# Moving the SBUF homes of a matmul kernel's operands: rows of 516 elements, and shifts of 4 to 192 bytes

## The chip, the cores and the metric

The kernel runs on 1 core of a Trainium2 chip. The metric is the device time of one execution in microseconds. Two runs of the kernel before took 1668.82 and 1669.12 us, median 1668.97 us.

## The reference

Two transformer blocks run one after the other on x (512 tokens, 1024 channels, fp32), two layers in each. What costs time is the projections, all of them matrix products of a 1024-channel (or 2816-channel) activation with fp32 weights:

```python
def conv_ffn(h, w_up, w_dw, b_dw, w_down):
    u = h @ w_up                      # 1024 -> 5632
    u = causal_dwconv(u, w_dw, b_dw)
    gate, val = jnp.split(u, 2, axis=-1)
    return (jax.nn.silu(gate) * val) @ w_down   # 2816 -> 1024

# first block, per layer l
h = rmsnorm(x, g_mix[l])
# layer 0: h @ w_in_a -> gated causal conv of 31 taps, layernorm, silu
# layer 1: h @ w_in_b, hk @ w_kvf -> attention with forget gates, 12 heads
# both: attention of 4 heads over a memory of 256 rows
x = x + jnp.concatenate([mix, mem_o], axis=-1) @ w_out[l]
x = x + conv_ffn(rmsnorm(x, g_ffn[l]), w_up[l], w_dw_f[l], b_dw_f[l], w_down[l])

# second block, per layer l
proj = jnp.einsum('bsd,de->bse', rmsnorm_2(x, pre_g[l]), w_in[l])
# -> a gated spatial mixing (8 heads) and grouped-query attention with rotary tables (8 heads)
x = x + rmsnorm_2(jnp.einsum('bse,ed->bsd', y, w_out[l]), post_g[l])
```

## The kernel before

**A unit.** All weights come as a stream of 255 units, each 128 partitions x 1024 fp32 elements (512 KB): eight blocks `k` of 128 x 128. A unit u lives in slot u % 4 (`SLOTS = 4`). SyncE loads it into `raw[slot]`, ScalarE rounds it to fp32r into `w_hi[slot]` (L674), GpSimd writes the rest `raw - w_hi` to `w_lo[slot]` (L591). The activations are split in the same way: `xs_hi` and `xs_lo` hold x's high and low part as `[128, 8, 512]` (ScalarE writes the one, VectorE the other), and `hid_hi` and `hid_lo`, `[128, 22, 512]`, hold the hidden layer of the feed-forward part.

**What TensorE does with a unit.** For each of the 8 blocks k it issues three matmuls into one PSUM bank (`products`, L1784): `w_hi` x hi (L1786), `w_hi` x lo (L1787) and `w_lo` x hi (L1788). In each, a weight load puts a 128 x 128 block of `w_hi` or `w_lo` into the array and the matmul streams 512 columns of the activation past it. So TensorE reads two operands of SBUF side by side: the streamed one of the running matmul, and the weight block of the next. 24 such pairs make a unit. `token_products` (L1832 to L1834) does the same with the roles turned: the weights are 128 columns of `xs_hi` or `xs_lo`, and 512 elements of `w_hi` or `w_lo` are streamed. The scores of the second block's attention (L1965, L1966) stream `k_hi` and `k_lo` past `q_stack`.

**Between the units.** Statistics (L1928), transposes (L1942, L1988, L2306), attention and the taps of the convolution (L2058) stand between units or between the blocks k of a unit, on the same TensorE queue, in an order written out by hand. SLOTS - 1 = 3 units are prepared ahead (`AHEAD`).

**Homes.** `put` places every tensor at a running byte address per partition (`cursor`), or at a given one. `LINE = 256`, and three places round the cursor to an address with the remainder of `xs_at` modulo 256: before `mem_kv1` and `k_hi`, and before `h0`, where the region with `hid_hi`, `mem_hi`, `q_stack` and the other stage buffers begins. By the program's addresses `xs_at` is 32896, remainder 128 modulo 256. Rows of 512 elements are 2048 bytes and slots are 4096 bytes, so that every row of `xs_hi`, `xs_lo`, `hid_hi`, `hid_lo`, `mem_hi`, `mem_lo`, `k_hi`, `k_lo` and `q_stack`, and every block of every `w_hi` and `w_lo` slot, begins at remainder 128. `sq_sum` (the weights of L1928) has remainder 0, and `cst` (the identity, the ones) 160.

Of the kernel before, what the change touches and what calls it, by code (L numbers as in the profile page):

```python
# [19 lines left out]
P = 128  # L20
T = 512
TM = 256
D = 1024
KT = D // P
# [13 lines left out]
UNIT = KT * P  # L38
SLOTS = 4
LINE = 256  # L40
AHEAD = SLOTS - 1
N_FOX = 12
N_MEM = 4
N_GQA = 8
# [65 lines left out]
FIRST_PARAMS = 2 * KT  # L110
N_CONSTS = 4 * P + 2 + N_FOX + Q

# [21 lines left out]
def two_blocks(nc, wstream, xT, memT, params, consts, rope, wsT, sbT, post_rows, out):  # L134
    f32, f32r, bf16 = mybir.dt.float32, mybir.dt.float32r, mybir.dt.bfloat16
# [7 lines left out]
    with ctx:  # L143

        start = (nc.sbuf_base + 31) // 32 * 32
        cursor = [start]

        def put(name, shape, dt, at=None):

            size = 4 if dt != bf16 else 2  # L150
            for n in shape[1:]:
                size *= n
            size = (size + 31) // 32 * 32
            where = cursor[0] if at is None else at
            if at is None:
                cursor[0] += size
            return nc.alloc_sbuf_tensor_at(name, shape, dt, offset=where)

        x = put("x", [P, KT, T], f32)
        xs_at = cursor[0]  # L160
        xs_hi = put("xs_hi", [P, KT, T], f32r)
        xs_lo = put("xs_lo", [P, KT, T], f32r)
        raw = [put(f"raw{s}", [P, UNIT], f32) for s in range(SLOTS)]
        w_hi = [put(f"w_hi{s}", [P, KT, P], f32r) for s in range(SLOTS)]
        w_lo = [put(f"w_lo{s}", [P, KT, P], f32r) for s in range(SLOTS)]
        fs_at = cursor[0]
        cursor[0] += 4 * (T + 8) * 4
        u_g = put("u_g", [P, T + 2], f32, fs_at)
# [30 lines left out]
        ident_b = put("ident_b", [P, P], bf16)  # L199
        mask_b = put("mask_b", [P, P], bf16)  # L200
        sel = put("sel", [P, N_FOX], f32r)
        h0 = cursor[0] + (xs_at - cursor[0]) % LINE

        def region():
            at = [h0]
# [15 lines left out]
        headsel = cst[:, 4 * P:4 * P + 2]  # L221
        gate_of = cst[:, 4 * P + 2:4 * P + 2 + N_FOX]
        fold = cst[:, 4 * P + 2 + N_FOX:4 * P + 2 + N_FOX + Q]

# [204 lines left out]
        def attention(name, heads, causal, q_of, k_of, v_of, pt, keys, gates, tile0, read, banks=tight):  # L429
            a = Attention()  # L430
            a.s, a.t, a.o = banks
            a.name, a.heads, a.causal, a.keys, a.gates, a.tile0 = name, heads, causal, keys, gates, tile0
            a.pts = pt
            a.q_of, a.k_of, a.v_of = q_of, k_of, v_of
            a.n = heads // 2 * QT
            a.i0 = sum(b.n for b in attentions)
            a.p0 = sum(b.heads // 2 for b in attentions)
            a.read, a.scale_rows, a.stacked = read, False, False
            attentions.append(a)
            return a  # L440
# [5 lines left out]
        def half(h):  # L446
            return slice(HD * (h % 2), HD * (h % 2) + HD)

        def mem_attention(name, qm, kv, vm, pt, read, banks=tight):
# [12 lines left out]
        att_f = attention(  # L462
            "fox", N_FOX, True,
            lambda h, qt: qf[half(h), h // 2, qt * P:(qt + 1) * P],
# [18 lines left out]
        def steps_in(j):  # L483

            first = KT * (j - ATT_FIRST)
            return [(STEP * s - first, s) for s in range(att_g[0].n + 2) if 0 <= STEP * s - first < KT]

        def b_block(i):

            return (att_m1, i) if i < att_m1.n else (att_f, i - att_m1.n)  # L490
# [97 lines left out]
        def _(pool):  # L588
            def low(s, u):
                pool.wait_ge(unit_hi, u + 1)  # L590
                nc.gpsimd.tensor_tensor(w_lo[s][:].rearrange("p k c -> p (k c)"), raw[s][:],  # L591
                                        w_hi[s][:].rearrange("p k c -> p (k c)").bitcast(f32),
                                        SUB).then_inc(unit_lo, 1)

            def scale_block(a, i):
                nk = keys_of(a, i % QT)
                b = a.i0 + i
                pool.wait_ge(at_inv, b + 1)
                for e in range(2):
                    n = 2 * (b % 2) + e  # L600
                    nc.gpsimd.tensor_scalar(prob[b % 2][:, e, 0:nk], prob[b % 2][:, e, 0:nk], rinv[:, n:n + 1],  # L601
                                            1.0, MUL, MUL).then_inc(at_p, 1)
# [5 lines left out]
            def lows(first, end):  # L608

                n = (end - first) // SLOTS  # L610
                if n >= 2:
                    with pool.Fori(0, n) as g:
                        for j in range(SLOTS):
                            low((first + j) % SLOTS, g * SLOTS + first + j)
                    first += n * SLOTS
                for u in range(first, end):
                    low(u % SLOTS, u)

            def diagonals(t):
                if t >= 2:  # L620
                    pool.wait_ge(part_up, NQ * (t - 1))
                n, w0 = PE_TAPS[t], PARAMS["w_dw_a"] + t * CW + DVE_TAPS[t]
                nc.gpsimd.tensor_tensor(diag[t % 2][:, 0:n, :], fold.unsqueeze(1).to_broadcast([P, n, Q]),
                                        par[:, w0:w0 + n].unsqueeze(2).to_broadcast([P, n, Q]),
                                        MUL).then_inc(diag_ok, 1)
# [12 lines left out]
            for j in range(2 * MT):  # L638
                low((U_GLU + j + AHEAD) % SLOTS, U_GLU + j + AHEAD)
                for k in range(KT):  # L640
# [3 lines left out]
                if 6 <= j < 10:  # L644
                    diagonals(j - 4)
            lows(U_MEM1 + AHEAD, U_B + AHEAD)
            for j in range(B_UNITS):
                low((U_B + j + AHEAD) % SLOTS, U_B + j + AHEAD)
                for k in range(KT):
                    for i in b_steps(j, k):  # L650
                        scale_block(*b_block(i))
            lows(U_OUT1 + AHEAD, U_IN2 + ATT_FIRST + AHEAD)
            for l in range(2):
                u0 = U_IN2 + l * L2_UNITS
                for j in range(ATT_FIRST, IN2_UNITS):
                    low((u0 + j + AHEAD) % SLOTS, u0 + j + AHEAD)
                    for _, i in steps_in(j):
                        if i < att_g[l].n:
                            scale_block(att_g[l], i)
                lows(u0 + IN2_UNITS + AHEAD, min(u0 + L2_UNITS + ATT_FIRST + AHEAD, UNITS))  # L660

# [1737 lines left out]
def _heads_by_pair(n_groups_first):  # L2399

    return [c for t in range(4) for h in (t, t + 4) for c in range(h * HD, (h + 1) * HD)]

def _stream(a):
    import numpy as np
    w_in = a["w_in_a"][0]
    kvf = a["w_kvf"]
    f = np.tile(np.concatenate([kvf[:, 2 * MIX:], np.zeros((D, P // 4 - N_FOX), kvf.dtype)], 1), 4)
    order = _heads_by_pair(4)
# [116 lines left out]
```

## Time and profile before

| | us |
|---|---|
| median of the 2 runs | 1668.97 |
| span of the profiled execution | 1667.2 |
| TensorE matmuls busy | 1636.4 |
| VectorE busy | 856.8 |
| ScalarE busy | 748.9 |
| GpSimd busy | 711.5 |

The mean granted clock of TensorE was 0.997 of full speed. A row of a group of instructions gives line, engine, operation, the tiles written and read (the streamed operand first, then the weights), the shape, the count, and then busy time and the mean length of one in ns. A matmul is 0.39 us long while the next one begins after 0.23 us: they overlap, so what TensorE's work costs is read from one start to the next, not from the length. "PEld" are the weight loads.

### The profile page before, as it was taken

What the parts mean: (1) busy time and instruction counts of PE and PEld (TensorE: products, weight loads), DVE (VectorE), ACT (ScalarE), POOL (GpSimd) and SP (SyncE); (2) the same over time, 40 slices, a digit from 0 to 9 for tenths busy, and PEclk for the clock granted to TensorE, in tenths of its full rate; (3) what the DMA queues carried; (4) which work ended last, traced back from release to release, by engine and by line L of the source; (5) the groups of instructions that cost most, each with busy time, mean ns of one, the idle gap of its engine ahead of it and who ended that gap; (6) DMA issues with size and microseconds to landing.
All of it is one profiled execution on the core that took longest, in us unless ns stands there. A gap on an engine that the chain in (4) does not pass through costs nothing.

```text
span 1667.2 us, 23890 instructions
## 1 busy us (share of the span) xinstructions
PE 1636.4 (98%) x8600; PEld 1290.4 (77%) x8600; DVE 856.8 (51%) x1431; ACT 748.9 (45%) x1189; POOL 711.5 (43%) x406
## 2 busy tenths in 40 slices
PE   8999999999999999999999999999999999999998
PEld 7656788888888877666888888888877778877776
DVE  7887545454431125434466666511365654566554
ACT  6433544444433235444445555423336643545641
POOL 4433334444444544443444444554424433435431
PEclk9999999999999999999999999999999999999999
DMA  7112123332233322111232233333321122311111
GB/s 254 65 52 65 60 92 101 101 100 91 89 112 113 101 90 76 52 52 37 79 113 91 92 94 101 114 101 113 121 75 51 56 72 64 130 66 51 64 55 60
DMA packets 40683, 144.29 MB, mean 87 GB/s; under 512 B 4640, under 2 KB 4640, under 8 KB 40608
## 3 DMA queue, kind: packets, MB, share of 16 engines
q1 hardware_dynamic: 39456, 139.59, 26.2%
q10 hardware_dynamic: 1152, 3.67, 0.7%
q8 instruction: 51, 0.84, 0.2%
q14 instruction: 24, 0.20, 0.0%
HBM read 141.14 MB, written 2.10 MB: 86 GB/s over the span
## 4 chain that ended last, share of the span: by engine, by line
PE 89%; DVE 5%; ACT 2%; issue 1%; DMA 1%; POOL 1%; SPq 0%; DVEq 0%; ACTq 0%; POOLq 0%
PE banks L1786 24%; PE banks L1788 23%; PE banks L1787 23%; PE banks L2005 3%; PE banks L1988 2%; PE banks L1833 2%; PE banks L1834 2%; PE banks L1832 2%; PE banks L2058 1%; PE banks L1970 1%; ACT prob L738 1%; DVE chain L1422 1%; PE banks L1965 1%; PE banks L1966 1%; DMA raw<-wstream 1%
## 5 line engine op out<-in xcount | busy, mean ns | idle before, releaser
L591 POOL TENSOR_TENSOR w_lo<-raw,w_hi 128x1024 fp32r<-128x1024 f32 x252 | 612.1, 2438 | 718.5 <-ACT w_hi L674 718.3
L1786 PE MATMUL banks<-xs_hi,w_hi 128*128 128x512 f32 (+2 forms) x1488 | 595.9, 400 | 4.1 <-DVE xs_lo L1484 1.6
L1788 PE MATMUL banks<-xs_hi,w_lo 128*128 128x512 f32 (+2 forms) x1488 | 577.2, 388 | 0.0
L1787 PE MATMUL banks<-xs_lo,w_hi 128*128 128x512 f32 (+2 forms) x1488 | 576.1, 387 | 0.0
L674 ACT ACTIVATE w_hi<-raw 128x1024 fp32r<-128x1024 f32 x255 | 263.9, 1053 | 267.0 <-PE banks L1788 221.6
L1786 PEld LDWEIGHTS banks<-xs_hi,w_hi 128*128 128x128 f32 x1488 | 280.2, 188 | 70.0 <-issue 15.7
L1788 PEld LDWEIGHTS banks<-xs_hi,w_lo 128*128 128x128 f32 x1488 | 279.7, 188 | 58.2
L1787 PEld LDWEIGHTS banks<-xs_lo,w_hi 128*128 128x128 f32 x1488 | 280.5, 189 | 53.7 <-issue 2.9
L601 POOL TENSOR_SCALAR prob<-prob,rinv 128x512 f32<-128x512 f32 (+3 forms) x144 | 92.3, 653 | 179.4 <-DVE rinv L1271 179.1
L1786 PE MATMUL banks<-hid_hi,w_hi 128*128 128x512 f32 x352 | 136.9, 389 | 0.0
L1787 PE MATMUL banks<-hid_lo,w_hi 128*128 128x512 f32 x352 | 136.9, 389 | 0.0
L1788 PE MATMUL banks<-hid_hi,w_lo 128*128 128x512 f32 x352 | 136.9, 389 | 0.0
L1335 DVE TENSOR_TENSOR x<-x,banks 128x512 f32<-128x512 f32 x16 | 11.0, 687 | 182.3 <-PE banks L1788 182.3
L1309 DVE TENSOR_TENSOR u_v<-banks,rstd 128x512 f32<-128x512 f32 x44 | 30.5, 692 | 127.2 <-PE banks L1788 127.2
L738 ACT ACTIVATE prob<-banks,nmax,head_r 128x512 f32<-128x512 f32 x64 | 49.2, 773 | 82.5 <-DVE nmax L1260 82.4
L780 ACT ACTIVATE t_v<-u_v,par 128x512 f32<-128x512 f32 x44 | 35.9, 816 | 102.5 <-DVE u_v L1309 102.5
L738 ACT ACTIVATE prob<-banks,nmax 128x256 f32<-128x256 f32 (+3 forms) x80 | 39.7, 502 | 88.0 <-DVE nmax L1263 87.8
L1788 PEld LDWEIGHTS banks<-hid_hi,w_lo 128*128 128x128 f32 x352 | 66.1, 188 | 13.8
L1786 PEld LDWEIGHTS banks<-hid_hi,w_hi 128*128 128x128 f32 x352 | 66.1, 188 | 13.7
L1787 PEld LDWEIGHTS banks<-hid_lo,w_hi 128*128 128x128 f32 x352 | 66.1, 188 | 13.6
L1988 PE MATMUL banks<-cst,prob 128*128 128x128 f32 x440 | 63.4, 278 | 4.3 <-POOL prob L601 3.9
L1988 PEld LDWEIGHTS banks<-cst,prob 128*128 128x128 f32 x440 | 48.8, 141 | 22.9 <-issue 12.4
(270 smaller groups left out, 1986.5 us busy)
## 6 DMA issues: line engine op xcount, KB each, us to landing
raw<-wstream SPq DMA_DIRECT2D x255, 512.0 KB, 3.5
x<-xT SPq DMA_DIRECT2D x4, 512.0 KB, 10.2
out<-pt SPq DMA_DIRECT2D x8, 256.0 KB, 2.0
memx<-memT SPq DMA_DIRECT2D x4, 256.0 KB, 5.0
ws_sb<-wsT ACTq DMA_DIRECT2D x2, 512.0 KB, 4.4
rope_sb<-rope ACTq DMA_DIRECT2D x2, 512.0 KB, 6.3
qk<-post_rows ACTq DMA_DIRECT2D x2, 512.0 KB, 3.6
sb_sb<-sbT ACTq DMA_DIRECT2D x2, 256.0 KB, 5.2
```

The costliest lines, as they stand in the source:

```text
L591: nc.gpsimd.tensor_tensor(w_lo[s][:].rearrange("p k c -> p (k c)"), raw[s][:], w_hi[s][:].rearrange("p k c -> p (k c)").bitcast(f32), SUB) ...
L601: nc.gpsimd.tensor_scalar(prob[b % 2][:, e, 0:nk], prob[b % 2][:, e, 0:nk], rinv[:, n:n + 1], 1.0, MUL, MUL).then_inc(at_p, 1)
L674: A(w_hi[s][:].rearrange("p k c -> p (k c)"), raw[s][:], ACT.Copy).then_inc(unit_hi, 1)
L738: A(prob[b % 2][:, e, 0:nk], a.s[b % len(a.s)][:, e, 0:nk], ACT.Exp, bias=nmax[:, n:n + 1], accum_out=rsum[:, n:n + 1], **kw).then_inc(at_ ...
L780: A(dst[:], src[:, 2:T + 2], ACT.Identity, scale=par[:, bass.ds(ch * 3 + (w0 + 2), 1)], bias=par[:, bass.ds(ch + b0, 1)]).then_inc(tap0, 1)
L1786: MM(dst, w_hi[slot][:, k, :], hi, start=start, stop=False)
L1787: MM(dst, w_hi[slot][:, k, :], lo, start=False, stop=False)
L1788: return MM(dst, w_lo[slot][:, k, :], hi, start=False, stop=stop)
L1832: MM(dst, hi, w_rows(w_hi, slot, half), start=start, stop=False)
L1833: MM(dst, lo, w_rows(w_hi, slot, half), start=False, stop=False)
L1988: last = nc.tensor.transpose(a.t[e][:, k * P:(k + 1) * P], prob[b % 2][:, e, k * P:(k + 1) * P], ident)
L2005: last = MM(a.o[n % len(a.o)][half(e), q0:T], a.v_of(2 * p + e, k), pt_of(a, p)[e][:, k, q0:T], start=(k == 0), stop=(k == nt - 1))
```

## The change

Only addresses change. Each row of `xs_hi` and `xs_lo` is allocated with 516 elements, of which 512 are used. The four `w_hi` slots become pieces of one tensor, moved by 0, 8, 64 and 128 bytes; those of `w_lo` by 0, 4, 128 and 192 bytes. The region with `hid_hi` and the stage buffers begins 64 bytes past the rounded address.

```diff
+HI_SHIFTS = (0, 8, 64, 128)
+LO_SHIFTS = (0, 4, 128, 192)
...
-        xs_hi = put("xs_hi", [P, KT, T], f32r)
-        xs_lo = put("xs_lo", [P, KT, T], f32r)
+        xs_hi = put("xs_hi", [P, KT, T + 4], f32r)[:, :, 0:T]
+        xs_lo = put("xs_lo", [P, KT, T + 4], f32r)[:, :, 0:T]
         raw = [put(f"raw{s}", [P, UNIT], f32) for s in range(SLOTS)]
-        w_hi = [put(f"w_hi{s}", [P, KT, P], f32r) for s in range(SLOTS)]
-        w_lo = [put(f"w_lo{s}", [P, KT, P], f32r) for s in range(SLOTS)]
+
+        def weight_slots(name, shifts):
+            cursor[0] += (xs_at - cursor[0]) % LINE
+            base = cursor[0]
+            whole = nc.alloc_sbuf_tensor_at(name, [P, SLOTS * UNIT + max(shifts) // 4], f32r, offset=base)
+            cursor[0] += SLOTS * UNIT * 4 + max(shifts)
+            firsts = [s * UNIT + shift // 4 for s, shift in enumerate(shifts)]
+            return [whole[:, at:at + UNIT].rearrange("p (k c) -> p k c", c=P) for at in firsts]
+
+        w_hi = weight_slots("w_hi", HI_SHIFTS)
+        w_lo = weight_slots("w_lo", LO_SHIFTS)
+        cursor[0] += -cursor[0] % 32
...
-        h0 = cursor[0] + (xs_at - cursor[0]) % LINE
+        h0 = cursor[0] + (xs_at + 64 - cursor[0]) % LINE
```

The instructions, their shapes, their order on each engine and their semaphores are those of before; each line number from 161 on grows (L1786 becomes L1798, L1787 L1799, L1788 L1800). The remainders of the addresses modulo 256, by the program's own addresses:

| operand | before | after |
|---|---|---|
| `xs_hi`, row k | 128 | 128 + 16 k |
| `xs_lo`, row k | 128 | 16 k |
| `w_hi`, slots 0 to 3 | 128 | 128, 136, 192, 0 |
| `w_lo`, slots 0 to 3 | 128 | 128, 132, 0, 64 |
| `hid_hi`, `hid_lo`, `mem_hi`, `mem_lo`, `q_stack`, `k_lo` | 128 | 192 |
| `k_hi`, `x`, `raw` | 128 | 128 |

## Rows read from the trace of the kernel before

**Rows 1.** The page's head and its row of busy time.

```profile
span 1667.2 us, 23890 instructions
PE 1636.4 (98%) x8600; PEld 1290.4 (77%) x8600; DVE 856.8 (51%) x1431; ACT 748.9 (45%) x1189; POOL 711.5 (43%) x406
```

**Rows 2.** The page's chain that ended last, by engine and by line.

```profile
PE 89%; DVE 5%; ACT 2%; issue 1%; DMA 1%; POOL 1%; SPq 0%; DVEq 0%; ACTq 0%; POOLq 0%
PE banks L1786 24%; PE banks L1788 23%; PE banks L1787 23%; PE banks L2005 3%; PE banks L1988 2%; PE banks L1833 2%; PE banks L1834 2%; PE banks L1832 2%; PE banks L2058 1%; PE banks L1970 1%; ACT prob L738 1%; DVE chain L1422 1%; PE banks L1965 1%; PE banks L1966 1%; DMA raw<-wstream 1%
```

**Rows 3.** TensorE's waits, longest first: us in total, times, longest.

```profile
PE banks L2090 <- ACT mem_hi L809: 6.8, 1, 6.8
PE banks L1988 <- POOL prob L601: 3.9, 8, 0.7
```

**Rows 4.** Matmul groups of the whole run by shape: count, busy us, mean ns.

```profile
L1788 PE MATMUL banks<-xs_hi,w_lo 128*128 128x512 f32 x1440 | 562.6, 391 | 0.0
L1787 PE MATMUL banks<-xs_lo,w_hi 128*128 128x512 f32 x1440 | 561.5, 390 | 0.0
L1786 PE MATMUL banks<-hid_hi,w_hi 128*128 128x512 f32 x352 | 136.9, 389 | 0.0
L1833 PE MATMUL banks<-w_hi,xs_lo 128*128 128x512 f32 x128 | 49.8, 389 | 0.0
L1966 PE MATMUL banks<-k_lo,q_stack 128*128 128x512 f32 x64 | 25.1, 392 | 0.0
```

**Rows 5.** Windows view, 300 to 560 us, and two groups within it.

```profile
300.00:560.00 260.00, 260.00 (x1149) 215.29 (x1148) 99.62 (x146) 100.14 (x126) 119.07 (x50) 1.00 0.31 99
...
L1787 PE MATMUL banks<-xs_lo,w_hi 128*128 128x512 f32 x249 | 96.9, 389 | 0.0
...
L1787 PE MATMUL banks<-hid_lo,w_hi 128*128 128x512 f32 x134 | 52.1, 389 | 0.0
```

**Rows 6.** Timeline of TensorE from 591 us: start, length, line.

```profile
591.03 0.39 PE L1786 MATMUL banks<-xs_hi,w_hi 128*128 128x512 f32 x1
591.26 0.39 PE L1787 MATMUL banks<-xs_lo,w_hi 128*128 128x512 f32 x1
591.49 0.40 PE L1788 MATMUL banks<-xs_hi,w_lo 128*128 128x512 f32 x1
591.72 0.95 PE L1928 MATMUL banks<-cst,sq_sum 128*128 128x1 f32 x8
...
592.85 0.39 PE L1787 MATMUL banks<-xs_lo,w_hi 128*128 128x512 f32 x1
...
594.00 0.40 PE L1786 MATMUL banks<-xs_hi,w_hi 128*128 128x512 f32 x1
594.24 0.39 PE L1787 MATMUL banks<-xs_lo,w_hi 128*128 128x512 f32 x1
594.46 0.40 PE L1788 MATMUL banks<-xs_hi,w_lo 128*128 128x512 f32 x1
...
595.15 0.39 PE L1788 MATMUL banks<-xs_hi,w_lo 128*128 128x512 f32 x1
```

**Rows 7.** Timeline of TensorE after the pause at 231 us.

```profile
231.44 0.39 PE L1787 MATMUL banks<-xs_lo,w_hi 128*128 128x512 f32 x1
...
231.67 0.40 PE L1788 MATMUL banks<-xs_hi,w_lo 128*128 128x512 f32 x1
231.91 0.39 PE L1786 MATMUL banks<-xs_hi,w_hi 128*128 128x512 f32 x1
232.13 0.39 PE L1787 MATMUL banks<-xs_lo,w_hi 128*128 128x512 f32 x1
...
233.99 0.28 PE L1928 MATMUL banks<-cst,sq_sum 128*128 128x1 f32 x2
```

**Rows 8.** Timeline and windows view at the lower clock, 65.2 to 67.2 us.

```profile
65.30 0.63 PE L1787 MATMUL banks<-xs_lo,w_hi 128*128 128x512 f32 x1
...
67.01 0.63 PE L1788 MATMUL banks<-xs_hi,w_lo 128*128 128x512 f32 x1
...
65.20:67.20 2.00, 2.00 (x6) 1.52 (x6) 1.81 (x4) 0.49 (x3) 0.00 (x0) 0.50 0.00 0
```

**Rows 9.** The page's groups of the two engines that write the weight slots.

```profile
L591 POOL TENSOR_TENSOR w_lo<-raw,w_hi 128x1024 fp32r<-128x1024 f32 x252 | 612.1, 2438 | 718.5 <-ACT w_hi L674 718.3
...
L674 ACT ACTIVATE w_hi<-raw 128x1024 fp32r<-128x1024 f32 x255 | 263.9, 1053 | 267.0 <-PE banks L1788 221.6
```

## Prediction

> **What bounds the kernel now.** I read the page's busy row first: TensorE's matmuls fill 1636.4 of 1667.2 us, the next engine only 856.8 [rows 1]. The chain that ended last agrees: 89% of the span is TensorE, and the three lines of `products` alone are 24 + 23 + 23 = 70% [rows 2]. TensorE's waits come third: its longest is 6.8 us, once, and the next adds up to 3.9 us in 8 times [rows 3]. So there is no wait to win or to create at first sight; what decides is how far apart two matmuls start. A change of that spacing is paid on the path almost in full, times the number of matmuls.
>
> The spacing has two regimes. In the undisturbed stretch from 300 to 560 us the window holds 260.00 us and 1149 matmuls (those cut by its edges counted in), which is 226.3 to 226.7 ns each, all 389 ns long, with `xs` and with `hid` alike [rows 5]. From 591.03 to 591.49 it is 0.46 / 2 = 230 by two digits, the same thing coarsely read. But behind an interruption the spacing is longer for a while: from 592.85 to 595.15 ten matmuls take 2.30 us, 230.0 ns each [rows 6], and from 231.44 to 233.99 eleven take 2.55 us, 231.8 ns each [rows 7]. Within these, single steps run from 0.22 us (231.91 to 232.13) to 0.24 us (231.67 to 231.91, 594.00 to 594.24), and the lengths from 0.39 to 0.40 us. Since length and spacing grow together, it is the streaming of the columns that is slowed, not the issue. The slots, the operands and the clock (full in the undisturbed window [rows 5]) are those of the fast regime, and all remainders are equal in both. What differs is the moment at which the two reads of SBUF run relative to each other. After some steps the spacing falls back to about 227 and stays there for hundreds of us.
>
> A second sign: at half clock (granted 0.50, the 1.2 GHz level) four steps take 67.01 - 65.30 = 1.71 us, 427 ns each [rows 8]. 512 columns at that clock are 426.7 ns, so nothing is lost there, while at full clock 226.7 is 13.3 ns more than the 213.3 of 512 columns. The loss appears only when both reads run at full rate.
>
> My reading: streamed rows and weight blocks share something in SBUF, the loss depends on how they meet, and with every remainder equal the stream of pairs settles in a repeating pattern at 226.7 ns, near the good end of what the trace shows (about 224 to 236).
>
> **The change part by part.** Nothing is added or removed: the same 8600 matmuls, the same order, DMAs and semaphores. Three effects are to be priced.
>
> (1) *The spacing of the 512-column fp32r matmuls.* There are 3 x 1440 with `xs`, 3 x 352 with `hid`, 3 x 128 with turned roles and 2 x 64 of scores, 5888 in all (one row of each kind stands in [rows 4]). Some run in the disturbed regime already. The mean lengths tell how many: with `hid` and in the turned form 389, as in the undisturbed stretch; with `xs`, unrounded, 561.5 / 1440 = 389.9 and 562.6 / 1440 = 390.7 ns [rows 4] against 96.9 / 249 = 389.2 [rows 5], 0.7 and 1.5 ns more, 1.1 on the mean. Disturbed steps average (2.55 + 2.30) / 21 = 231.0 ns [rows 6, 7], 4.3 over 226.7. So 1.1 / 4.3 = 26% of the 4320 are disturbed, 3200 are not; with 1056 + 384 and half of the 128 scores, 4700 matmuls are in the good pattern. After the change the difference of remainders changes with k, with the slot and between `w_hi` and `w_lo`, so no two successive pairs meet alike and there is no single pattern to settle in. I take for them the mean of the wandering steps, 231.0: 4700 x 4.3 ns = 20.2 us. Bounds from the rows: all at the shortest step, 224 (0.22 in [rows 7]), 5888 x -2.7 = -16 us; all at the longest, 236 (0.235 to 0.24), 4700 x 9.3 = +44 us. A bound further off is no loss at all, 427 / 2 = 213.4 ns from the half clock [rows 8]: 5888 x -13.3 = -78 us. I take the wandering mean because it is measured on these very shapes at full clock; the half clock is a state the kernel is hardly in.
>
> The premise that remainders matter has one thin piece of evidence. At 591.49, out of the good pattern, the matmul beside which the weights of L1928 are read (`sq_sum`, remainder 0, the others 128) is 0.40 long instead of 0.39 [rows 6]. The weights there are plain fp32 as well, so it could be the type.
>
> (2) *Writes to moved addresses.* ScalarE's 1053 ns and GpSimd's 2438 ns per unit are 3.5 us, in series [rows 9], against 24 x 226.7 = 5.44 us of TensorE per unit, with three units ahead. GpSimd idles 718.5 us before this very line [rows 9]. Cost 0, hidden behind TensorE's unit. It would end only if GpSimd's subtraction grew beyond 5.4 us, 2.2 times its present length; no row shows a start off a 16-byte boundary on any engine, and a copy of the same bytes is the nearest row. The same slack makes the splits of `xs` harmless in the dense stretches; at the edges of stages a tenth more on 8 writes would be below 1 us.
>
> (3) *Blocks that straddle a boundary.* Slots moved by 4 or 8 bytes (one in four of each kind) touch one more piece of memory per block of 512 bytes: at most 1 in 32 pieces more to read, on a weight load whose 188 ns fit into the spacing. I take 0.
>
> Sum, against the profile's own time: 1667.2 + 20.2 = 1687.4 us. The median of the runs is 1.8 us above that span, so 1689 us, 1.2% slower.
>
> The Trainium skill speaks against this. "TensorE: Matmul & The Clock Gate", "Step-by-step: what each phase is for", says that the streamed operand and the weight load have read ports of their own and that loading the next weights takes nothing from the running matmul. By that, addresses would not matter and the time would be 1669. The same page ("Phases on the wall clock") has 215.7 ns between 512-column matmuls; this trace shows 226.7, 11 ns more in a stream with a weight load beside each matmul. The trace disagrees with the page at full clock and would agree with it at half clock, which is why I don't follow it.
>
> **The rivals.**
>
> *A. Addresses don't matter.* The two regimes come from moments alone, the pattern at 226.7 is found again whatever the remainders: 1669 us, plus or minus 3. For it: the one sign of a remainder above is also a change of type. 
> *B. The new pairs meet badly most of the time.* Remainders open relations that this trace does not contain, and many pairs sit at 235 to 236 for whole units: from 234 ns on (+7.3 x 4700 = 34 us) the result is over 2% slower; at 236 it is 1667.2 + 44 + 1.8 = 1713 us. For it: steps of 0.24 exist [rows 6, 7]. Against: they never repeat in the trace, a short step follows. 16%.
>
> *C. The new pairs meet well, the kernel gets faster.* The good pattern of now still loses 13.3 ns per matmul; if equal remainders are what makes both reads want the same piece of memory, spreading them takes loss away. From below 226 ns on the mean it decides for faster; at 224 throughout it gives 1669 - 16 = 1653 us, half of the loss gone (220 ns) gives 5888 x 6.65 = 39 us, 1630 us. For it: the half clock shows that streaming without loss exists. Against: the shortest of the steps in the trace is 224, so over 2% needs spacings never seen at full clock. 11%, of which 5% beyond 2%.
>
> **How the numbers follow.** The forecast (1675 to 1702 us) has 50%, A 23%, B 16%, C 11%. The range from 1665 to 1712 holds the forecast, nearly all of A and most of B, 8 in 10; it leaves out C and the tail of B. The three chances go by 2% of the time (33 us), taken as about what a measurement of this kernel can tell from no change: faster 5%, the far part of C; slower 16%, B; within 2%, the other 79%.
>
> **What would show it.** In the window from 300 to 560 us the count of matmuls should fall from 1149 to about 1126 (260 / 0.231), and the mean lengths of L1798 to L1800 rise from 389 to about 393 ns, with several different lengths from matmul to matmul instead of one. If A is right, count and lengths are unchanged; if C, the lengths are below 389. ScalarE's and GpSimd's writes should keep 1053 and 2438 ns, and TensorE's waits stay below 10 us each; a wait of TensorE for `w_lo` would show part (2) wrong. The prediction fails if the mean spacing in that window is not between 229 and 233 ns.

## The result and the profile after

| | before | after |
|---|---|---|
| median of the 2 runs, us | 1668.97 | 1688.53 |
| span of the profiled execution, us | 1667.2 | 1686.8 |
| mean granted clock | 0.997 | 0.999 |

The ratio is 1.012, with a 95% interval of 1.0104 to 1.0136: 1.2% slower, clearly different from no change, and below the 2% of the three chances. The prediction was 1689 us, with a range of 1665 to 1712.

The page after, its busy row (which answers to [rows 1]) and its chain by engine ([rows 2]):

```profile
PE 1656.4 (98%) x8600; PEld 1290.1 (76%) x8600; DVE 824.9 (49%) x1431; ACT 749.2 (44%) x1189; POOL 686.9 (41%) x406
...
PE 91%; DVE 4%; ACT 2%; issue 1%; POOL 0%; DMA 0%; DVEq 0%; ACTq 0%; POOLq 0%
```

The matmuls are busy for 20.0 us more, in the same number, and the span is 19.6 us longer; no other engine's busy time grew by more than 0.3 us. VectorE's fell from 856.8 to 824.9 us, 29.9 of it on two of its lines (L1313 and L1317). VectorE doesn't bound the kernel, and why these two got shorter was not isolated. TensorE's waits are as short as in [rows 3]; the two longest after:

```profile
PE banks L2102 <- ACT mem_hi L821: 6.0, 1, 6.0
PE banks L2000 <- POOL prob L613: 4.2, 9, 0.7
```

The windows view of 300 to 560 us, with two of its groups. As in [rows 5], the first bracket holds the number of matmuls, and the 1.00 near the end is the granted clock:

```profile
300.00:560.00 260.00, 260.00 (x1127) 211.35 (x1126) 100.36 (x147) 99.14 (x125) 112.28 (x49) 1.00 0.31 98
...
L1799 PE MATMUL banks<-xs_lo,w_hi 128*128 128x512 f32 x252 | 99.0, 393 | 0.0
...
L1799 PE MATMUL banks<-hid_lo,w_hi 128*128 128x512 f32 x124 | 48.6, 392 | 0.0
```

1127 matmuls instead of 1149 in the same 260 us, 393 and 392 ns long instead of 389. Read as the prediction read the 1149, that is a mean step of 230.7 to 231.1 ns, inside its 229 to 233. In the timeline of that stretch the starts no longer come at equal steps: 0.23 us from 300.61 to 300.84, but 0.24 from 302.46 to 302.70, with lengths of 0.39 and 0.40 mixed, as in [rows 6, 7] behind an interruption:

```profile
300.61 0.39 PE L1799 MATMUL banks<-xs_lo,w_hi 128*128 128x512 f32 x1
300.84 0.39 PE L1800 MATMUL banks<-xs_hi,w_lo 128*128 128x512 f32 x1
...
302.23 0.40 PE L1800 MATMUL banks<-xs_hi,w_lo 128*128 128x512 f32 x1
302.46 0.40 PE L1798 MATMUL banks<-xs_hi,w_hi 128*128 128x512 f32 x1
302.70 0.40 PE L1799 MATMUL banks<-xs_lo,w_hi 128*128 128x512 f32 x1
```

The groups of the whole run, against [rows 4]:

```profile
L1800 PE MATMUL banks<-xs_hi,w_lo 128*128 128x512 f32 x1440 | 566.4, 393 | 0.0
L1799 PE MATMUL banks<-xs_lo,w_hi 128*128 128x512 f32 x1440 | 566.4, 393 | 0.0
...
L1798 PE MATMUL banks<-hid_hi,w_hi 128*128 128x512 f32 x352 | 138.4, 393 | 0.0
...
L1845 PE MATMUL banks<-w_hi,xs_lo 128*128 128x512 f32 x128 | 50.5, 394 | 0.0
```

Their busy times tell where the time came from, since a matmul that is longer by some ns also moves the next start by about as many (in the window 389 to 393 ns of length, 226.7 to about 231 of step). `xs` x `w_lo` has 566.4 - 562.6 = 3.8 us more, `xs_lo` x `w_hi` 566.4 - 561.5 = 4.9, the third group (L1786, now L1798, from 580.9 to 584.7) 3.8: 12.5 us. The three `hid` groups have 4.2 us more, the three with turned roles 2.2. That is 18.9 of the 19.6 us.

GpSimd's subtraction, [rows 9], got shorter, from 2438 to 2339 ns, and moved nothing, since it waits for ScalarE:

```profile
L603 POOL TENSOR_TENSOR w_lo<-raw,w_hi 128x1024 fp32r<-128x1024 f32 x252 | 587.1, 2339 | 756.6 <-ACT w_hi L686 756.5
```

### The profile page after: what moved, and what is told of

Its sections match the earlier page's. It is cut to its first block, busy times and chain, and to the rows that moved or that the text cites. A ratio compares the mean times of both kernels' runs of the same rounds, so it can differ in the third digit from the quotient of the medians.

```text
span 1686.8 us, 23890 instructions
## 1 busy us (share of the span) xinstructions
PE 1656.4 (98%) x8600; PEld 1290.1 (76%) x8600; DVE 824.9 (49%) x1431; ACT 749.2 (44%) x1189; POOL 686.9 (41%) x406
## 4 chain that ended last, share of the span: by engine, by line
PE 91%; DVE 4%; ACT 2%; issue 1%; POOL 0%; DMA 0%; DVEq 0%; ACTq 0%; POOLq 0%
PE banks L1798 24%; PE banks L1800 24%; PE banks L1799 24%; PE banks L2017 3%; PE banks L2000 2%; PE banks L1846 2%; PE banks L1844 2%; PE banks L1845 2%; PE banks L2070 1%; PE banks L1982 1%; ACT prob L750 1%; DVE chain L1434 1%; PE banks L1977 1%; PE banks L1978 1%; DVE banks L1434 1%
## 5 line engine op out<-in xcount | busy, mean ns | idle before, releaser
L603 POOL TENSOR_TENSOR w_lo<-raw,w_hi 128x1024 fp32r<-128x1024 f32 x252 | 587.1, 2339 | 756.6 <-ACT w_hi L686 756.5
L1798 PE MATMUL banks<-xs_hi,w_hi 128*128 128x512 f32 (+2 forms) x1488 | 599.8, 403 | 3.8 <-DVE xs_lo L1496 1.6
L1800 PE MATMUL banks<-xs_hi,w_lo 128*128 128x512 f32 (+2 forms) x1488 | 581.1, 391 | 0.0
L1799 PE MATMUL banks<-xs_lo,w_hi 128*128 128x512 f32 (+2 forms) x1488 | 581.0, 390 | 0.0
L686 ACT ACTIVATE w_hi<-raw 128x1024 fp32r<-128x1024 f32 x255 | 263.9, 1053 | 274.1 <-PE banks L1800 227.7
L1798 PEld LDWEIGHTS banks<-xs_hi,w_hi 128*128 128x128 f32 x1488 | 279.9, 188 | 74.1 <-issue 15.5
L1800 PEld LDWEIGHTS banks<-xs_hi,w_lo 128*128 128x128 f32 x1488 | 279.5, 188 | 62.7
L1799 PEld LDWEIGHTS banks<-xs_lo,w_hi 128*128 128x128 f32 x1488 | 280.1, 188 | 58.3 <-issue 2.9
L1800 PE MATMUL banks<-hid_hi,w_lo 128*128 128x512 f32 x352 | 138.6, 394 | 0.0
L1798 PE MATMUL banks<-hid_hi,w_hi 128*128 128x512 f32 x352 | 138.4, 393 | 0.0
L1799 PE MATMUL banks<-hid_lo,w_hi 128*128 128x512 f32 x352 | 137.9, 392 | 0.0
L1799 PEld LDWEIGHTS banks<-hid_lo,w_hi 128*128 128x128 f32 x352 | 66.1, 188 | 15.4
L1800 PEld LDWEIGHTS banks<-hid_hi,w_lo 128*128 128x128 f32 x352 | 66.1, 188 | 15.2
L1798 PEld LDWEIGHTS banks<-hid_hi,w_hi 128*128 128x128 f32 x352 | 66.1, 188 | 14.7
```

Source lines behind the costliest of these rows:

```text
L686: A(w_hi[s][:].rearrange("p k c -> p (k c)"), raw[s][:], ACT.Copy).then_inc(unit_hi, 1)
L1798: MM(dst, w_hi[slot][:, k, :], hi, start=start, stop=False)
L1799: MM(dst, w_hi[slot][:, k, :], lo, start=False, stop=False)
L1800: return MM(dst, w_lo[slot][:, k, :], hi, start=False, stop=stop)
```

## The experiments

All kernels are the one before with other homes; none leaves work out. The measured quantity beside the time is the mean length of a 512-column matmul in the window of 300 to 560 us: 389 there means a step of 226.7 ns, and each ns of length is about a ns of step. "Difference" is how many bytes the streamed row begins past the weight block it meets, modulo 256; before the change it is 0 for all of these matmuls.

The expectations weigh these explanations against each other. V is the prediction's own: differences that vary keep the pairs from settling. N: any difference other than 0 costs. S: starts off a 16-byte boundary cost. D: the cost depends on the difference alone. H: the homes of before are special as such. W: it is the weight blocks' start that costs.

### One part of the change at a time

Rows of 516 alone:

```diff
-        xs_hi = put("xs_hi", [P, KT, T], f32r)
-        xs_lo = put("xs_lo", [P, KT, T], f32r)
+        xs_hi = put("xs_hi", [P, KT, T + 4], f32r)[:, :, 0:T]
+        xs_lo = put("xs_lo", [P, KT, T + 4], f32r)[:, :, 0:T]
```

> Only the rows of xs_hi and xs_lo are 516 elements long; slots and hid stay at remainder 128. Theory V (a loss comes from differences of remainders that vary from pair to pair, so that no pattern can repeat): the xs matmuls rise from 389.2 in the dense window to about 393 ns, hid stays at 389; 3500 matmuls x 4.3 ns = +15 us, 1684. Rival S (starts off a 16-byte boundary cost, rows of 2064 bytes being whole 16-byte pieces): 1669, nothing. Rival N (any difference from zero costs, constant or not): as V here.

1686.30 us, ratio 1.0106 (1.0089 to 1.0123). The window's groups:

```profile
L1801 PE MATMUL banks<-xs_lo,w_hi 128*128 128x512 f32 x252 | 99.2, 394 | 0.0
...
L1801 PE MATMUL banks<-hid_lo,w_hi 128*128 128x512 f32 x125 | 48.6, 389 | 0.0
```

V and N had 1684 us, S 1669. In one trace, the matmuls whose streamed operand was moved are at 393 to 394 and those whose streamed operand was not are at 389 as before. Addresses matter (rival A of the prediction falls). All starts here are on 16-byte boundaries, so rival S alone doesn't explain it either.

Slots alone (at the addresses that the diff's shifts give, rows of 512, `h0` as before):

```diff
+HI_SHIFTS = (0, 8, 64, 128)
+LO_SHIFTS = (0, 4, 128, 192)
```

> Only the slots are moved, w_hi by 0, 8, 64, 128 and w_lo by 0, 4, 128, 192; xs rows 512, hid not moved. Within a unit the difference now takes two values in turn, one for w_hi and one for w_lo. Theory V: no settled pattern in slots 1 to 3, which is three quarters of 4700 x 4.3 ns, +15 us, 1684, xs and hid alike at about 392. Rival S: only slot 1 is off a 16-byte boundary, a quarter, +5 us or less. Rival N: slots 1 to 3 again, +15 us.

1686.38 us, ratio 1.0104 (1.0088 to 1.0121), as V and N had it; S had at most 5 us. xs is at 392 to 394, hid too:

```profile
L1801 PE MATMUL banks<-xs_lo,w_hi 128*128 128x512 f32 x253 | 99.2, 392 | 0.0
...
L1800 PE MATMUL banks<-hid_hi,w_hi 128*128 128x512 f32 x124 | 48.8, 394 | 0.0
```

The hid region alone:

```diff
-        h0 = cursor[0] + (xs_at - cursor[0]) % LINE
+        h0 = cursor[0] + (xs_at + 64 - cursor[0]) % LINE
```

> Only the region with hid is moved by 64 bytes: during the 1056 matmuls with hid the difference is a constant 64. Theory V: a constant difference lets the pattern settle; 1669, hid at 389 or another single length. Rival N: every hid matmul loses about 4 ns, hid mean 393, +4 us, 1673. Rival S: 1669, hid 389.

1670.69 us, ratio 1.0013 (1.0004 to 1.0023). The window:

```profile
L1801 PE MATMUL banks<-xs_lo,w_hi 128*128 128x512 f32 x247 | 96.1, 389 | 0.0
L1800 PE MATMUL banks<-hid_hi,w_hi 128*128 128x512 f32 x135 | 53.2, 394 | 0.0
L1802 PE MATMUL banks<-hid_hi,w_lo 128*128 128x512 f32 x134 | 52.5, 392 | 0.0
L1801 PE MATMUL banks<-hid_lo,w_hi 128*128 128x512 f32 x134 | 52.0, 388 | 0.0
```

With hid the pairs do settle, in a repeating group of three: 394, 392, 388, mean 391.3, 2.3 ns over 389. 1056 x 2.3 = 2.4 us against a measured 1.9. So a constant difference can settle, as V says, but at another level and in three lengths, which V had left open.

The three parts don't add: 17.5 + 17.6 + 1.9 = 37 us, and all three together cost 19.6. Rows alone and slots alone each already put the xs matmuls at 392 to 394, and doing both puts them at 393: the loss is a level that is reached, not a toll per edit.

### Four constant differences side by side

`w_hi` and `w_lo` of a slot are moved alike, and each slot has its own name, so that the groups of one trace are an experiment each:

```diff
+HI_SHIFTS = (0, 4, 8, 16)
+LO_SHIFTS = (0, 4, 8, 16)
```

> w_hi and w_lo of one slot are moved alike, slots by 0, 4, 8, 16 bytes, and carry names of their own (a to d), so that one run gives four constant differences side by side. Theory V: each slot settles at a single length after a few matmuls, a at 389, the others possibly at another, and the whole is within 5 us of 1669 unless the settled value is another. Rival N: a 389, b, c and d about 393. Rival S: b and c (4 and 8 bytes) longer, d (16) at 389.

1688.23 us, ratio 1.0117 (1.0097 to 1.0137). Window groups, slots a to d:

```profile
L1800 PE MATMUL banks<-xs_hi,w_hi_d 128*128 128x512 f32 x64 | 25.4, 398 | 0.0
...
L1800 PE MATMUL banks<-xs_hi,w_hi_b 128*128 128x512 f32 x64 | 25.2, 394 | 0.0
...
L1800 PE MATMUL banks<-xs_hi,w_hi_a 128*128 128x512 f32 x64 | 25.0, 390 | 0.0
...
L1800 PE MATMUL banks<-xs_hi,w_hi_c 128*128 128x512 f32 x59 | 23.2, 392 | 0.0
```

Within units of constant difference, 4, 8 and 16 bytes cost 4, 2 and 8 ns on this line, and slot a, with difference 0, is back at 390 between them. V falls in its strict form: it isn't the variation that costs, the 24 pairs of one slot meet alike and still lose. N (each non-zero difference costs) is right here, though the costs differ; S falls too, since slot d, on a 16-byte boundary, is the worst. The sign of the difference has to be kept in what follows: here the weights lie past the row, so these are differences of -4, -8 and -16.

With shifts of (0, 32, 64, 128) and hid moved by 160:

> Slots a to d moved by 0, 32, 64, 128 bytes, hid region by 160: eight constant differences at once, for xs 0, 32, 64, 128, for hid 160, 128, 96, 32. Theory D: each has its own mean between 226 and 233 ns (length 388.5 to 396), a with xs lowest at 389 to 390, 64 near 391. A difference below 389 would be a faster home. Rival N: all but a with xs at 393.

1692.92 us, ratio 1.0147 (1.0127 to 1.0167). Slot a with xs: 389 to 390. All seven other differences: 392 to 396, none below 389. In the window:

```profile
L1800 PE MATMUL banks<-xs_hi,w_hi_a 128*128 128x512 f32 x64 | 24.9, 389 | 0.0
L1801 PE MATMUL banks<-xs_lo,w_hi_c 128*128 128x512 f32 x61 | 24.1, 396 | 0.0
...
L1800 PE MATMUL banks<-hid_hi,w_hi_a 128*128 128x512 f32 x28 | 11.1, 396 | 0.0
```

One expectation was missed: "64 near 391". Slot c with xs is at 395 to 396. The 391.3 came from the hid region moved by 64, where the row lies 64 past the weights; here the weights lie 64 past the row, which modulo 256 is another difference (192).

With shifts of (160, 192, 224, 240) and hid moved by 192:

> Slots a to d moved by 160, 192, 224, 240 bytes, hid region by 192: constant differences for xs of 160, 192, 224, 240, for hid of 32, 0, 32 the other way and 48. Theory D: hid with slot b (difference 0) at 389 to 391 though both stand 192 bytes from xs; the others between 389 and 396. Rival H (the homes of before are special): hid with slot b no lower than the rest.

1689.71 us, ratio 1.0128 (1.0107 to 1.0148). The window:

```profile
L1801 PE MATMUL banks<-xs_lo,w_hi_a 128*128 128x512 f32 x64 | 25.5, 399 | 0.0
...
L1802 PE MATMUL banks<-xs_hi,w_lo_b 128*128 128x512 f32 x64 | 25.2, 394 | 0.0
...
L1801 PE MATMUL banks<-xs_lo,w_hi_b 128*128 128x512 f32 x64 | 25.1, 392 | 0.0
...
L1800 PE MATMUL banks<-xs_hi,w_hi_d 128*128 128x512 f32 x64 | 24.9, 389 | 0.0
...
L1800 PE MATMUL banks<-hid_hi,w_hi_b 128*128 128x512 f32 x30 | 11.7, 389 | 0.0
L1801 PE MATMUL banks<-hid_lo,w_hi_b 128*128 128x512 f32 x30 | 11.7, 389 | 0.0
```

hid with slot b, both 192 bytes past their old homes (remainder 64), is at 389: the homes of before are nothing special (rival H falls), two operands moved by the same 192 bytes are as good. And slot d with xs, whose weights begin 16 bytes before the streamed row modulo 256 (difference 16), is at 389 to 390, as good as equal homes. Slot b with xs has the difference of 64 with the sign that hid had above, and is at 389, 392 and 394, the same three levels. The rest is at 392 to 399, three ns above what was expected for the worst.

### The same constant difference everywhere

```diff
+HI_SHIFTS = (192, 192, 192, 192)
+LO_SHIFTS = (192, 192, 192, 192)
```

> All slots are moved by 192 bytes, so that xs and hid alike stand 64 bytes before or 192 behind the weights modulo 256, everywhere and constantly, which is the difference that hid had in the run with hid alone moved (64). Theory D with a period of 256 bytes: the three repeating steps of 231.7, 229.1 and 225.9 ns found there, mean 228.9, now on 4700 matmuls: 4700 x 2.2 = +10 us, 1679. Rival N (any difference costs 4 to 5 ns): 1688. If the period isn't 256: another pattern, between 224 and 236.

1679.91 us, ratio 1.0070 (1.0053 to 1.0087), against 1679 expected. The hid groups:

```profile
L1800 PE MATMUL banks<-hid_hi,w_hi 128*128 128x512 f32 x129 | 50.8, 394 | 0.0
L1802 PE MATMUL banks<-hid_hi,w_lo 128*128 128x512 f32 x129 | 50.6, 392 | 0.0
L1801 PE MATMUL banks<-hid_lo,w_hi 128*128 128x512 f32 x129 | 50.1, 388 | 0.0
```

394, 392, 388 again, the group of three of the run with hid alone moved by 64. There the streamed row began 64 bytes past the weights, here the weights begin 192 past the row: the same modulo 256. So the pattern depends on the difference modulo 256 (or a divisor of it; against 128 speaks slot c of the shifts 0 to 128, at 395 to 396 with a difference of 192), and its cost grows with the matmuls that have it: 4700 x 2.3 = 10.8 us against a measured 11.4, with the turned roles now unequal too.

### Both operands moved alike, off a boundary

```diff
-        xs_hi = put("xs_hi", [P, KT, T], f32r)
-        xs_lo = put("xs_lo", [P, KT, T], f32r)
+        def moved(name):
+            whole = put(name, [P, KT * T + 1], f32r)
+            return whole[:, 1:1 + KT * T].rearrange("p (k t) -> p k t", t=T)
+
+        xs_hi = moved("xs_hi")
+        cursor[0] += (xs_at - cursor[0]) % LINE
+        xs_lo = moved("xs_lo")
...
+HI_SHIFTS = (4, 4, 4, 4)
+LO_SHIFTS = (4, 4, 4, 4)
```

> xs_hi, xs_lo and all weight slots begin 4 bytes past their homes of before, off every 16-byte boundary, but alike: the difference of remainders is 0 for xs. hid stays, so that with hid the difference is a constant 4 bytes. Theory D (only the difference of the two homes counts): xs settles at 389 and 226.7 ns again, hid is near the 232.4 of the slot moved by 4, 1056 x 5.7 = +6 us, 1675. Rival S (the boundary counts): xs near 232, +20 us and more. Rival H (the homes of before are special as such): the same as S.

1714.66 us, ratio 1.0277 (1.0260 to 1.0294), the slowest of all. The window:

```profile
L1805 PE MATMUL banks<-xs_hi,w_hi 128*128 128x512 f32 x256 | 102.7, 401 | 0.0
L1806 PE MATMUL banks<-xs_lo,w_hi 128*128 128x512 f32 x256 | 102.4, 400 | 0.0
...
L1806 PE MATMUL banks<-hid_lo,w_hi 128*128 128x512 f32 x111 | 43.7, 394 | 0.0
```

Theory D was wrong: with equal remainders 4 bytes off, xs is at 397 to 401, 11 ns over 389 and worse than with any unequal pair above, while hid, streamed from its old home past weights moved by 4, is at 394 as slot b was, as expected, and there the difference is constant over the whole stretch. Of the rivals S comes nearest, with over twice its price. A boundary counts besides the difference. Which boundary, and is it the streamed row's? The next two runs ask this. First the same kernel with 16 instead of 4 bytes:

> xs_hi, xs_lo and all slots 16 bytes past their homes of before, alike; hid stays. Theory D16 (the difference counts, and besides it a streamed row that begins off a 16-byte boundary costs more): xs settles at 389 and 226.7 again; hid, whose weights now stand 16 bytes past it, is near the 233.3 of the slot moved by 16, 1056 x 6.6 = +7 us, 1676. Rival B32 (the boundary is 32 bytes or more): xs loses as with 4 bytes, near 238, 1710 and more.

1691.90 us, ratio 1.0145 (1.0129 to 1.0160). The window:

```profile
L1806 PE MATMUL banks<-xs_lo,w_hi 128*128 128x512 f32 x253 | 99.7, 394 | 0.0
...
L1805 PE MATMUL banks<-hid_hi,w_hi 128*128 128x512 f32 x122 | 48.2, 395 | 0.0
```

For xs neither expectation holds; hid (394 to 397) is where it was expected. xs does not return to 389 (theory D16), nor is it near 400 (B32): 393 to 394. 16 bytes are better than 4, but not a boundary on which equal homes are good; the good pairs of equal homes in these runs stand at remainders of 128 and 64, both multiples of 64. Whether equal homes 32 bytes off would do was not tried. With unequal ones a row at remainder 32 was no worse than others: hid in the run with shifts of 0 to 128 stood there, and with slots b and d it is at 394 to 396, as xs is at remainder 128 with the same differences of 128 (394 to 395) and 32 (394 to 396, slot c of the shifts 160 to 240).

Then the streamed rows of xs alone moved by 4, the slots left at their homes (shifts of 0):

> Only xs_hi and xs_lo begin 4 bytes later; slots and hid as before. Theory D16: the cost of an unaligned streamed row shows by itself, xs at 397 to 401 (mean spacing 235 to 238), hid untouched at 389; about 3500 to 4000 matmuls x 10 ns = +38 us, 1707. Rival W (it was the weight blocks off the boundary that cost, or both together): xs near 393, +17 us, 1686.

1708.08 us, ratio 1.0236 (1.0220 to 1.0251), 1707 expected. The window:

```profile
L1807 PE MATMUL banks<-xs_hi,w_lo 128*128 128x512 f32 x258 | 103.4, 401 | 0.0
...
L1805 PE MATMUL banks<-hid_hi,w_hi 128*128 128x512 f32 x113 | 44.0, 389 | 0.0
```

xs is at 400 to 401 as in the run before last, with weights on their boundary: it is the streamed row, and rival W falls. Weight blocks moved by 4 under an aligned streamed row cost 5 ns (394), a streamed row moved by 4 costs 11 to 12.

### The weights 16 bytes before the rows

```diff
+HI_SHIFTS = (240, 240, 240, 240)
+LO_SHIFTS = (240, 240, 240, 240)
```

> All slots moved by 240 bytes, that is the weights begin 16 bytes before the streamed rows modulo 256, for xs and hid. By the slot with this difference in the run before (its spacings were mostly 226 and 227, mean 227.9, among slots that had disturbed it) it should settle at 226.7 or a trifle lower: 1669 within 3 us. If the difference of 0 is the only good one: 1680 and more.

1672.42 us, ratio 1.0023 (1.0014 to 1.0032), 0.4 us outside the expected 1669 within 3. In the window xs and hid are at 389 and the count is 1149, exactly as before; that part was right. The rest is in the whole run's groups of turned roles, where these same homes are streamed. The window, then the groups:

```profile
300.00:560.00 260.00, 260.00 (x1149) 215.29 (x1148) 99.89 (x146) 100.37 (x127) 119.32 (x50) 1.00 0.33 100
...
L1801 PE MATMUL banks<-hid_lo,w_hi 128*128 128x512 f32 x352 | 136.9, 389 | 0.0
...
L1846 PE MATMUL banks<-w_hi,xs_hi 128*128 128x512 f32 x128 | 51.3, 401 | 0.0
L1847 PE MATMUL banks<-w_hi,xs_lo 128*128 128x512 f32 x128 | 51.2, 400 | 0.0
```

Same two remainders, 128 and 112: streamed from 128 past weights at 112 it is 389, streamed from 112 past weights at 128 it is 400 to 401. 51.3 + 51.2 + 51.2 against 50.0 + 49.8 + 49.8 is 4.1 us, enough for all of the 3.7 us lost.

Only `w_lo` moved by 240:

> Only the w_lo slots are moved by 240 bytes, so that of three pairs two have difference 0 and one 16 (the weights 16 bytes before). If each pair's loss were its own, 226.7 throughout and 1669; if the pattern of three pairs counts as a whole, a repeating group of three different spacings with a mean between 226 and 231, 1669 to 1690.

1669.70 us, ratio 1.0007 (0.9997 to 1.0017), no difference shown. xs and hid at 389, so the pairs of a repeating group need not have the same difference, if each is a good one. Only `w_lo` streamed is longer, 396 against 389, 0.9 us on 128 matmuls, as much as the medians differ by:

```profile
L1848 PE MATMUL banks<-w_lo,xs_hi 128*128 128x512 f32 x128 | 50.7, 396 | 0.0
```

No run was faster than before, so there is no better version to show from these.

## Why the prediction was right, and where not

*What bounds the kernel.* Right: TensorE's step, paid on the path. 20.0 us more busy time gave 19.6 us more span.

*The count and the price of part (1).* Right within its rounding. 4.3 ns on 4700 matmuls, 20.2 us, against 18.9 us by the groups: xs 13.8 predicted and 12.5 measured, hid 4.5 and 4.2, turned roles 1.7 and 2.2. The window held 1127 matmuls where about 1126 was written, the lengths were 392 to 394 where 393 was. What made the number good was to take the price from this trace's own disturbed stretches at the same shapes and clock (231.0), not from either bound: 16 us faster or 44 us slower. The faster bound stood on less than the prediction says: a step that reads 0.22 occurs in the quiet stretch too (340.57 to 340.79 us), where 226.7 is printed as 0.23, 0.23, 0.22, so the row of [rows 7] does not show a step of 224.

*The mechanism given for it.* Right that the homes of the two reads decide. Wrong in "no single pattern to settle in" as the cause: constant differences of 4, 8, 16 and 32 bytes lose as much as the varying ones do (392 to 398), inside a unit and, for 4 bytes, over the whole stretch of hid (394). Varying and constant differences both end near 393 because most pairs of homes are at 392 to 396, and 389 is the exception. So the step that led to the price, that only unsettled pairs lose, did not hold, and that the mean of the disturbed steps fitted all the same was in part luck. A reason may be that those steps and these pairs sample the same levels; that is an inference from their equal means, not something a run isolated.

*Part (2), the writes.* Right that they cost nothing: ScalarE's 1053 ns stayed, GpSimd's shortened by 4%. The prediction named only a growth as possible.

*Part (3), straddling.* Half wrong. It looked at the weight blocks only and took 0. The weight blocks moved by 4 or 8 are indeed no worse than other moved ones (394 and 392), but where the roles are turned those slots are streamed, and a streamed row costs by itself when it is unaligned (11 ns at 4 bytes). In the run with shifts of 0, 4, 8 and 16 the slot moved by 4 is at 398 to 401 when streamed, the one not moved at 391 to 395. In this change that is slot 1 of the turned groups alone, so it is contained in their 2.2 us.

*The rivals.* A fell with the run of rows alone (394 beside 389 in one trace). B's price exists, but not in this change: it came with streamed rows moved by 4 bytes (400, 1708 and 1715 us), and on 384 matmuls with streamed rows at remainder 112 past weights at 128 (400), which is on a 16-byte boundary. C didn't show in any time: in twelve more placements no group of these matmuls was below 388, and the one at 388 stands in a group of three whose mean is 391.

*The evidence for it.* The prediction called the 0.40 at 591.49 thin, since the type changed too. The trace of before has six places where this line comes right before L1928; five read 0.40 and one 0.39 (829.30 us), and one of the five lies in a disturbed stretch. That doesn't part the type from the remainder, no run isolated it, and it stays open.

*The rules weighed against the trace.* The Trainium skill's "TensorE: Matmul & The Clock Gate", "Step-by-step: what each phase is for", gives the streamed operand and the weight load independent read ports. By that rule the time would have been 1669; the trace disagrees by 19.6 us here and by 46 us in the worst placement. The Trainium skill's "SBUF — State Buffer", "Specifications (TRN2)", says that SBUF has lines of 16 bytes and that each cross to a new one pays a penalty, whose size it doesn't give. A row of 2048 bytes that begins 4 bytes late crosses 1 line more in 128; as an estimate from that page's line and this trace's step, if the whole step were such crossings, that is 226.7 / 128, under 2 ns. Measured were 11. And a start moved by 16 crosses none more and still cost 4 to 5 ns. The trace agrees with that page in that a start off a 16-byte line costs, not in the size, and not in that a start on one is free.

## What to carry to other kernels

Where TensorE streams fp32r rows with a weight load beside each matmul, give streamed rows and weight blocks homes whose remainder modulo 256 is equal and a multiple of 64 (128 and 64 are the two that were measured as good here, 132 and 144 as bad), and keep row pitches a multiple of 256 bytes, so that the remainder stays; other types and shapes were not tried. A pad of 4 elements per row cost 1.1% here, and a start 4 bytes late 2.4%. Compare start-to-start steps and mean lengths of one shape between a quiet stretch and the steps behind an interruption: their difference is the price of losing the good pattern. Parts of such a change must be measured together, since their losses don't add.

## What the runs showed of the hardware that was not expected

The two operands of a matmul are not alike. The same two homes (remainders 128 and 112) gave 389 ns in one role and 400 in the other, and 4 bytes under the streamed row cost 11 ns where 4 bytes under the weights cost 5. What unit of SBUF stands behind this, and why weights 16 bytes before the row are as good as equal ones (389) and weights 16 bytes past it the worst of the small shifts (394 to 398), no run tells.

GpSimd's subtraction `raw - w_hi` into `w_lo` got faster when `w_hi` and `w_lo` were moved by 4 or 8 bytes. From the whole run with slots moved by 0, 4, 8 and 16 bytes, `raw` not moved:

```profile
L605 POOL TENSOR_TENSOR w_lo_a<-raw,w_hi_a 128x1024 fp32r<-128x1024 f32 x64 | 156.2, 2440 | 177.9 <-ACT w_hi_a L688 177.9
L605 POOL TENSOR_TENSOR w_lo_d<-raw,w_hi_d 128x1024 fp32r<-128x1024 f32 x63 | 152.3, 2417 | 198.8 <-ACT w_hi_d L688 198.7
L605 POOL TENSOR_TENSOR w_lo_c<-raw,w_hi_c 128x1024 fp32r<-128x1024 f32 x63 | 128.2, 2035 | 212.0 <-ACT w_hi_c L688 212.0
L605 POOL TENSOR_TENSOR w_lo_b<-raw,w_hi_b 128x1024 fp32r<-128x1024 f32 x62 | 125.2, 2019 | 189.8 <-ACT w_hi_b L688 189.8
```

2440 and 2417 ns at 0 and 16 bytes, 2019 and 2035 at 4 and 8: 16 to 17% less. With both slots moved by 4 everywhere it was 2032 on the mean of all 252. In the change itself one slot of four is moved so (8 and 4 bytes), which fits the 4% on its mean. It is worth nothing in this kernel, where GpSimd waits for ScalarE for 718.3 us before and 756.5 after, and ScalarE's copy into the same slots did not change (1052 to 1055 ns in all four).
